# One place per unit for the attention's small products, in the first and third mixed layer

## What is computed

```python
q = rms_norm(q, gq); k = rms_norm(k, gk)
for gi, (window, dilation) in enumerate(((128, 1), (512, 4), (2048, 16))):
    o, l = _dilated_group(q[:, :, sl], k[:, :, sl], v[:, :, sl], window, dilation)
wts = jax.nn.softmax(jnp.stack(lses, axis=0), axis=0)
o = jnp.sum(wts[..., None] * jnp.stack(outs, axis=0), axis=0)
```

## Time and profile before

| | |
|---|---|
| median of 3 runs | 2347.3 us (2346.65 to 2347.45) |
| the profiled execution | 2347.8 us, of which the span from first to last instruction is 2346.0 us |
| TensorE busy | 2318.4 us, 99% of the span |
| its weight loads | 1952.9 us, 83% |
| DVE busy | 1639.3 us, 70% |
| ACT busy | 1022.4 us, 44% |
| Pool busy | 159.8 us, 7% |
| mean granted clock of TensorE | 0.999 of full speed |
| chain that ended last | TensorE 88%, DVE 5%, ACT 3%, Pool 2% |

### The profile page before, as it was taken

One profiled execution on the slowest core, in us unless ns is written; L12 is line 12 of the kernel. 1 busy time (PEld: TensorE's weight loads), 2 busy tenths in 40 slices (PEclk: granted clock), 3 DMA queues, 4 the chain that ended last, 5 costly groups with the idle time before them and its releaser, 6 DMA issues.

```text
span 2346.0 us, 35328 instructions
## 1 busy us (share of the span) xinstructions
PE 2318.4 (99%) x14380; PEld 1952.9 (83%) x14380; DVE 1639.3 (70%) x2344; ACT 1022.4 (44%) x1511; POOL 159.8 (7%) x196
## 2 busy tenths in 40 slices
PE   8999999999999999999999999999999999999999
PEld 6877778787888999877778999988888888789998
DVE  7666556878668777676667877766755557687774
ACT  5434463447244343356655433443423234543332
POOL 5111110000000000062120000000000000100000
PEclk9999999999999999999999999999999999999999
DMA  4222213222323333321022333322222212233322
GB/s 161 74 73 64 73 47 111 79 73 73 99 90 108 101 107 108 108 72 55 28 91 91 116 100 102 105 81 90 75 70 81 90 54 72 90 126 108 108 92 71
DMA packets 60674, 206.31 MB, mean 88 GB/s; under 512 B 7249, under 2 KB 7249, under 8 KB 60386
## 3 DMA queue, kind: packets, MB, share of 16 engines
q1 hardware_dynamic: 59760, 202.93, 27.3%
q10 hardware_dynamic: 754, 1.14, 0.2%
HBM read 201.94 MB, written 2.10 MB: 87 GB/s over the span
## 4 chain that ended last, share of the span: by engine, by line
PE 88%; DVE 5%; ACT 3%; POOL 2%; issue 1%; DMA 0%; POOLq 0%; SPq 0%; DVEq 0%; ACTq 0%
PE psum L1973 41%; PE psum L2387 7%; PE psum L2388 7%; PE psum L2386 7%; PE psum L2343 5%; PE psum L2345 5%; PE psum L2344 5%; POOL arena L714 1%; DVE wlo L1177 1%; PE psum L2138 1%; PE psum L2034 1%; ACT whi L766 1%; PE psum L2091 1%; PE psum L2109 1%; PE psum L2000 1%
## 5 line engine op out<-in xcount | busy, mean ns | idle before, releaser
L766 ACT CAST whi<-raw 128x1024 fp32r<-128x1024 f32 (+1 forms) x399 | 400.0, 1005 | 467.9 <-PE psum L1973 191.8
L1177 DVE TENSOR_TENSOR wlo<-raw,whi 128x1024 fp32r<-128x1024 f32 (+1 forms) x399 | 466.2, 1168 | 62.3 <-ACT whi L766 61.5
L1973 PE MATMUL psum<-hhi,whi 128*128 128x512 f32 x872 | 347.4, 398 | 10.8 <-DVE wlo L1177 8.8
L1973 PE MATMUL psum<-hlo,whi 128*128 128x512 f32 x872 | 345.3, 396 | 0.0
L1973 PE MATMUL psum<-hhi,wlo 128*128 128x512 f32 x872 | 343.3, 394 | 0.0
L2388 PE MATMUL psum<-hhi,wlo 128*128 128x512 f32 x768 | 299.7, 390 | 0.0
L2387 PE MATMUL psum<-hlo,whi 128*128 128x512 f32 x768 | 299.6, 390 | 0.0
L2386 PE MATMUL psum<-hhi,whi 128*128 128x512 f32 x768 | 299.1, 389 | 0.0
L1973 PE MATMUL psum<-uhi,whi 128*128 128x512 f32 x624 | 247.6, 397 | 0.0
L1973 PE MATMUL psum<-ulo,whi 128*128 128x512 f32 x624 | 246.1, 394 | 0.0
L1973 PE MATMUL psum<-uhi,wlo 128*128 128x512 f32 x624 | 244.7, 392 | 0.0
(11 more groups left out here) (309 smaller groups left out, 4265.5 us busy)
## 6 DMA issues: line engine op xcount, KB each, us to landing
raw<-in_packed_dram SPq DMA_DIRECT2D x359, 512.0 KB, 3.5
raw<-in_packed_dram SPq DMA_DIRECT2D x40, 256.0 KB, 2.6
x<-in_xt_dram SPq DMA_DIRECT2D x8, 256.0 KB, 5.4
out_dram<-x SPq DMA_DIRECT2D x8, 256.0 KB, 2.0
arena<-in_near_bias_dram ACTq DMA_DIRECT2D x1, 1024.0 KB, 6.3
vec<-in_vec_dram ACTq DMA_DIRECT2D x1, 44.0 KB, 4.0
arena<-in_gla_gate_up_dram ACTq DMA_DIRECT2D x1, 32.0 KB
arena<-in_gla_gate_bias_dram ACTq DMA_DIRECT2D x1, 2.0 KB
```

The lines of the kernel that those rows point to most:

```text
L766: nc.scalar.copy(whi[:, u % 4, 0:kt, :], raw[:, u % 4, 0:kt, :]).then_inc(hi_done, 1)
L1177: dve.tensor_tensor(wlo[:, u % 4, 0:kt, :], raw[:, u % 4, 0:kt, :], whi[:, u % 4, 0:kt, :].bitcast(F32), ALU.subtract).then_inc(lo_done, 1)
L1973: mm = pe.matmul(g, w[:, u % 4, k, :], v[:, k, :], start=n == 0, stop=n == 3 * kt - 1)
```

## The change

`static` gets a flag `together`. It is true where more than one entry stands in `between`, no gated linear attention is in the unit, the first entry isn't a norm and the layer isn't the second mixed one. Then all entries are issued one behind the other at one place, given by `meet`: half of the products if `both` is true or `lead` is 0, and `lead` otherwise. For 24 products the places 6, 12, 18 become 6; 10, 14, 19 become 10; 4, 16, 18, 21 become 12; 8, 16 become 12. Only TensorE's order changes.

```diff
+            def meet(total, lead, both):
+                return total // 2 if both or not lead else lead
...
+                    together = len(between) > 1 and not soon and between[0][0] != "norm" and name != "l2"
                     for i, part in enumerate(between):
                         if u is not None:
-                            products(u, mark(i, n, total, lead, both), mark(i + 1, n, total, lead, both), *operand)
+                            if not together:
+                                products(u, mark(i, n, total, lead, both), mark(i + 1, n, total, lead, both), *operand)
+                            elif i == 0:
+                                products(u, 0, meet(total, lead, both), *operand)
                         PARTS[part[0]](*part[1:])
                     if u is not None:
-                        products(u, mark(n - 1, n, total, lead, both), total, *operand)
+                        begun = meet(total, lead, both) if together else mark(n - 1, n, total, lead, both)
+                        products(u, begun, total, *operand)
```

## The result

The change makes the kernel slower by 1.6%: 2385.3 us, the median of five runs (2383.1 to 2385.6), against 2347.3; ratio 1.0159, 95% interval 1.0146 to 1.0172. The forecast was 2382. The profiled execution took 2385.5 us, its span is 2383.7, 37.7 longer than before. Times in this text are medians of executions; one execution of `turns_only`, which took 3283 us at a mean granted clock of 0.66, is left out.

The account below looks back on a forecast made before the run. TensorE was taken as the bound. 26.5 + 2.7 + 1.6 - 1.0 + 0.4 = +30.2, plus 5 for the clock, made +35 on the profiled 2347.8; with the median 0.5 lower, forecast 2382 us, range 2364 to 2394.

Parts of the forecast that it names:

- What bounds the kernel, and what sets the time of the weights: Attention: TensorE bounds; weights come from a DVE, ACT, Pool chain, fixed against unit 12's start at 12.96 us.
- the one wait of this kind is in unit 16: Attention: DVE waits for the scores only in unit 16, at 123.16, 6.55 us after the unit's start.
- Part 1: Attention: weights' transposes moved earlier wait for Pool; +26.5 us over three patterns, +2.7 in units 39, 41 and 43.
- Part 2: Units 7, 16, 25, 34: head sum and V transposes share a PSUM bank; +1.6 us, in unit 7 only.
- Part 3: 22 places where products between two small groups go away; only 7 give anything, 0 to 1.5 us, taken as -1.0.
- Part 4: Third mixed layer: earlier variance sums cost nothing, their input being ready; unit 322 costs more; +0.4 us.
- The term of unit 322: Third mixed layer: last head's step 2 moves from product 4 to 6, lengthening a TensorE wait of 0.73; 0.455 us.
- Part 5: Units 13, 15 and their likes: granted clock falls behind three of six new waits, 1.7 us each; +5 us.
- A: Units 13, 15 and their likes: DVE's L1320 goes ahead of Pool, 1.2 us later in six units; 2389, 7%.
- B: Attention: the clock falls at every new wait over 1.2 us, 15 times; 2403, 6%.
- C: Attention: weights move earlier with the scores, so only the transposes' extra move counts, no fall; 2365, 12%.
- D: Attention: weights aren't late at all and 22 joins give 2.2 to 4.6 us; 2344, 3%.

Follow-up runs that it names:

- turns_only: Kernel before, with only the transposes of the attention weights (the turns) moved earlier as in the change; 2386.6 us, ratio 1.0167.
- after_recip_first: The change, with DVE's reciprocal of the sums ahead of the evacuation of the unit before; 2354.1 us, ratio 1.0028.
- turn_mid: The change, but the weights' transposes stand after 12 products (14 behind V transposes) instead of 6 (10); 2361.0 us, ratio 1.0059.
- head_sum_apart: The change, but in units 7, 16, 25 and 34 the head sum stays at product 4; 2375.6 us, ratio 1.0122.
- best: Kernel before, with scores, use, V transposes joined, weights' transposes mostly late, head sums at 4, third-layer variance sums earlier except unit 322, DVE's reciprocal first; 2340.9 us.
- before_recip_first: Kernel before, with DVE's reciprocal ahead of the evacuation and nothing else; 2345.5 us, ratio 0.9989.
- l3_only: Kernel before, with the change in the third mixed layer alone; 2347.7 us in a single execution.
- joins_only: Kernel before, with first-layer scores, use and V transposes joined, weights' transposes left late, four head sums at product 4; 2342.6 us, ratio 0.9981.

## Why the prediction was right, and where it wasn't

- **What bounds the kernel, and what sets the time of the weights.** Right. The weights' time against the pair's start stood at 9.73, 12.93, 13.12 and 14.90 us where 9.74, 12.96, 13.50 and 14.88 were taken. That "the one wait of this kind is in unit 16" was misread: DVE waited for the scores in unit 14 too, 0.25 us, and that is why the third came 0.4 early. `turns_only` and `after_recip_first` show from two sides that it is this chain: moving the turns alone gives the cost, taking 1.5 us out of the chain takes 31 of the 38 us away.
- **Part 1, +26.5 and +2.7.** Right: the patterns' 26.0 without falls, and 3.1 in units 37, 39, 41 and 43 (0.1 of it in unit 37, which was given none), less 0.6 of joins between them, 2.4 in all. `turn_mid` has the slope: fewer products of move, as much less wait.
- **Part 2, +1.6.** Right for unit 7 (1.67). "In the other three it lies inside the wait of part 1" was true of the sum and misleading as a cause; part 1 had the late L1320 in its 6.5 us and put no price on it. `head_sum_apart` shows 1.6 us in each of them: the head sum's late place is why Pool ends at 14.9 there in spite of the earlier scores. The change could have had 6.5 us back by leaving four head sums alone.
- **Part 3, -1.0.** Right for the change, where the turns' waits eat most joins: 0.3 in units 18, 27 and 36, 0.6 in 38, 40 and 42. The price of a join stands at the upper end of what I gave: 0.18 to 0.24 us between scores and use, where the bound was 0.21. When I put the same reasoning to the joins alone, it failed (1.6 expected, 4.6 measured in the layer), because I held Pool's end fixed where DVE had waited for the scores, and left out the 0.32 us that the turn of unit 13 had to spare.
- **Part 4, +0.4.** The term of unit 322 is right in size (0.46), though it came as a new wait of the variance sum and not in the 0.73 of L1337. "So nothing" for the variance sums was wrong: the step asked whether TensorE would wait for their input, not who waits for their output. The layer gave -0.24.
- **Part 5, +5.** The mechanism is right, and the number low: five falls at 1.56 us, 7.8, where three at 1.7 were taken. This is most of the 3 us by which 2382 missed. The rows couldn't give the number of falls, and the same waits had two in `head_sum_apart`: that the forecast came so near is in part luck.
- **Rivals.** A (DVE's L1320 ahead of Pool) didn't happen: L680 takes 2.37 in unit 13 as before, and it is L1320 that takes longer, 1.94 us (1.76 before, 1.16 without Pool beside it). The Trainium skill's rule (SBUF — State Buffer, "Who interferes with whom"), that issue order decides who blocks, is borne out by `after_recip_first`: with L1177 first Pool takes 2.37 us, with Pool first 1.47, and L1177 takes 2.12 instead of 1.20. B (a fall at every wait over 1.2 us) is out: none of the waits of 1.2 to 1.5 us has one. C (the weights move with the scores) is false in unit 12, a quarter true in unit 14 (0.4 of 1.4 us) and true in unit 16 once the head sum is out of the way. D would have needed 2.4 us. `best` gets there another way, by leaving the turns late.

## What to carry to other kernels

A small product that waits for a chain on other engines stands best where its data lands. Before moving it forward, read the end of the last step against the start of the unit, and what that step's own queue makes it wait for; moving the first link of the chain helps only where that link is what the queue waits for. Joining scores and use saved 0.2 us a unit on TensorE and is worth it for groups whose data is there, and two steps that share a bank through another engine don't belong side by side.

## What the runs showed of the hardware

Whether the clock falls behind a wait isn't settled by the wait's length alone. In the second mixed layer all kernels have the same wait of 2.1 us but `turn_mid`, where it was 1.46 and had no fall. In six profiles (before, the change, `turns_only`, `before_recip_first`, `l3_only`, `best`) the granted clock was 0.5 for 3.4 us behind it, in three (`joins_only`, `head_sum_apart`, `after_recip_first`) it stayed at 1.0. In the attention, five of six waits of 2.4 to 2.5 us had a fall in the change and two of six in `head_sum_apart`. In `turns_only` a wait of 2.29 us had none and one of 2.13 had one. All falls lasted 3.4 us and began between 0.15 us before the wait's end and 1.6 us behind it; none came with a wait under 2.1. What decides between them stays open. A fall cost 1.6 us in the attention and 1.1 in the second mixed layer, and by so much two executions of one kernel can differ.
